# Two-block transformer kernel: order of loads, place of selection rounds and form of the reciprocals in the layer attention

## The reference

```python
h = rms_norm(x); proj = h @ w_in                       # 1024 x 3528
mixed = concat(retention(ret_cols),                    # 4 heads, chunkwise, with a norm and a gate
               dsa(dsa_cols),                          # 4 heads
               dilated(dil_cols))                      # 8 heads
x = x + mixed @ w_out
x = x + square(relu(rms_norm(x) @ w_up)) @ w_down

# dsa: every query attends to the 128 keys with the best index score
logits = einsum('bqhd,bsd->bqhs', q_idx, k_idx)        # 8 index heads
score  = einsum('bqhs,bqh->bqs', relu(logits), w_idx)  # causal mask after it
_, idx = top_k(score, 128)
p = softmax(q @ k[idx] * 64 ** -0.5); o = p @ v[idx]
```

## Time and profile before

| what | us |
|---|---|
| median of three runs | 3216.89 |
| profiled execution | 3215.07 |
| its span | 3213.0 |
| TensorE matmul busy | 2753.3 (86%) |
| VectorE busy | 1742.8 (54%) |
| ScalarE busy | 1271.9 (40%) |
| first layer of the second block: index sums to end of projections | about 1700 to 1857 |
| its layer attention, first scores | 1873.7 |

### The profile page before, as it was taken

How to read it: one execution, slowest core, us unless ns; L and a number is a source line. 1 busy time by engine, 2 the same in 40 slices (tenths; PEclk the granted TensorE clock), 3 DMA queues, 4 the chain that set the end, 5 groups by cost and what they waited for, 6 DMA issues and landing times. The chain is left out here.

```text
span 3213.0 us, 34356 instructions
## 1 busy us (share of the span) xinstructions
PE 2753.3 (86%) x11967; PEld 2064.3 (64%) x11967; DVE 1742.8 (54%) x2583; ACT 1271.9 (40%) x1739; POOL 114.6 (4%) x172
## 2 busy tenths in 40 slices
PE   3879989978798399999489969899999996989998
PEld 0167566556577277777376746688877573668886
DVE  1045146667575588888635755444443665544444
ACT  1033246656522177777433245222233314532222
POOL 2011000000000100000000100000000100000000
PEclk9989999989999699999779979899997997989999
DMA  8655343245253299999622442122222234222221
GB/s 316 217 159 151 114 109 91 81 103 129 90 180 118 111 354 371 386 371 366 232 61 82 118 109 85 62 95 91 91 87 63 92 99 129 65 66 92 95 100 72
DMA packets 241592, 466.35 MB, mean 145 GB/s; under 512 B 67864, under 2 KB 90640, under 8 KB 241455
## 3 DMA queue, kind: packets, MB, share of 16 engines
q1 hardware_dynamic: 226383, 413.73, 39.2%
q0 software_dynamic: 15072, 50.87, 4.7%
HBM read 399.83 MB, written 64.72 MB: 145 GB/s over the span
## 5 line engine op out<-in xcount | busy, mean ns | idle before, releaser
L1803 DVE TENSOR_TENSOR WL<-W,WH 128x2048 fp32r<-128x2048 f32 x131 | 300.2, 2292 | 502.2 <-ACT WH L1275 497.0
L1275 ACT ACTIVATE WH<-W 128x2048 fp32r<-128x2048 f32 x131 | 250.4, 1912 | 649.8 <-PE BKP L736 590.1
L736 PE MATMUL BKP<-hH,WH 128*128 128x512 f32 x896 | 357.4, 399 | 15.8 <-DVE hL L2201 13.2
L736 PE MATMUL BKP<-hL,WH 128*128 128x512 f32 x896 | 352.7, 394 | 0.0
L736 PE MATMUL BKP<-hH,WL 128*128 128x512 f32 x896 | 352.7, 394 | 0.0
L736 PE MATMUL BKP<-WH,aH 128*128 128x512 f32 (+1 forms) x544 | 215.3, 396 | 22.5 <-DVE aL L2396 10.4
L736 PE MATMUL BKP<-WL,aH 128*128 128x512 f32 (+1 forms) x544 | 211.4, 389 | 0.0
L736 PE MATMUL BKP<-WH,aL 128*128 128x512 f32 (+1 forms) x544 | 211.3, 388 | 0.0
L736 PEld LDWEIGHTS BKP<-hH,WH 128*128 128x128 f32 x896 | 171.4, 191 | 57.1 <-issue 20.3
L736 PE MATMUL BKP<-WH,hH 128*128 128x512 f32 (+3 forms) x512 | 201.2, 393 | 7.2 <-ACT Z L1326 3.1
L736 PE MATMUL BKP<-WH,hL 128*128 128x512 f32 (+3 forms) x512 | 194.2, 379 | 0.0
(11 more groups left out here) (443 smaller groups left out, 5581.1 us busy)
## 6 DMA issues: line engine op xcount, KB each, us to landing
W<-in_w_expert_gu_dram SPq DMA_DIRECT2D x46, 1024.0 KB, 8.7
G<-in_w_expert_gu_dram SPq DMA_DIRECT2D x46, 1024.0 KB, 8.9
W<-in_w_in_dram SPq DMA_DIRECT2D x42, 1024.0 KB, 5.4
W<-in_w_up_dram SPq DMA_DIRECT2D x32, 1024.0 KB, 5.4
W<-in_w_down_dram SPq DMA_DIRECT2D x32, 1024.0 KB, 5.0
W<-in_w_expert_down_dram SPq DMA_DIRECT2D x24, 1024.0 KB, 8.0
G<-in_w_expert_down_dram SPq DMA_DIRECT2D x22, 1024.0 KB, 8.0
X<-in_w_in_dram SPq DMA_DIRECT2D x16, 1024.0 KB, 8.2
```

The costliest lines, as they stand in the source:

```text
L736: mm = pe.matmul(BK[j][:, 0:cols], lt, rh, start=start and a == 0, stop=stop and a == len(q) - 1, skip_group_check=True)
L1275: act.activation(WH[s][:], W[s][:], ACT.Copy).then_inc(sems["w_hi"], 1)
L1803: v.tensor_tensor(WL[s][:], W[s][:], WH[s][:].bitcast(F32), ALU.subtract).then_inc(sems["w_lo"], 1)
```

## The change

Four edits, all in the second block's layers:

1. SyncE's wait for the stores moves from the front of `mixed_heads` to behind the loads of the first two heads, in front of the two w_out loads. What the first heads load was stored long before, and retention's own loads have waited for it.
2. ScalarE rounds the first head (`mixed_rounded(0)`) during the evacuation of the last projection unit, in front of the copy of part 2. A tiny exponential in front of it brings the table of the exponential in at that place. VectorE makes that head's remainders (`mixed_remainders(0)`) in front of `selected(3)`. `sel_done` goes: TensorE's first scores don't need the selection, and VectorE, which adds the mask, has made it itself.
3. Eight rounds of tile 2 move behind the index sums 16 to 23. In the loop of 24 steps there remain eight rounds of tile 2 (steps 0 to 7) and 16 of tile 3 (steps 8 to 23), one a step.
4. VectorE writes a head's reciprocals out as 64 equal columns (two copies), for both heads side by side. TensorE spreads them once for a pair, after the second head's product, with 128 weight columns.

```diff
-TOP_2 = [2, 2, 1, 2, 1, 2, 2, 1, 2, 1]
-TOP_3 = [1] * 12 + [2] * 2
+TOP_2 = [1] * 8
+TOP_3 = [1] * 16
...
+        TINY = F[:, 1, 16:17]
+        RDW = [AT[:, c:c + 256].rearrange("p (t s c) -> p t s c", t=2, s=2) for c in (512, 1280)]
...
             def after_retention(s):
-                if s == 0:
-                    for b in range(3):
-                        sp.wait_ge(sems[f"st_written{b}"], T.next(f"st_written{b}", stored(STORES_2, b)))
-                        sp.sem_inc(sems["paused"], 1)
                 sp.wait_ge(sems["ret_oe"], T.next("ret_oe", NT))
...
                 for s in range(2):
                     values(4 + s, s)
+                for b in range(3):
+                    sp.wait_ge(sems[f"st_written{b}"], T.next(f"st_written{b}", stored(STORES_2, b)))
+                    sp.sem_inc(sems["paused"], 1)
                 for u in range(2):
                     load(WOR[u], out_unit(wo, 0, u), ...)
...
-                    pe.wait_ge(sems["head_rd"], T.next("head_rd"))
-                    for tt in range(NT):
-                        mm = pe.matmul(RD2[rows, tt * P:(tt + 1) * P], RDS[:, s, tt:tt + 1].to_broadcast([P, HD]), IDN[:], ...)
+                    if s == 1:
+                        pe.wait_ge(sems["head_rd"], T.next("head_rd", 2))
+                        for tt in range(NT):
+                            mm = pe.matmul(RD2[:, tt * P:(tt + 1) * P], RDW[tt // 2][:, tt % 2, :, :]..., IDN[:], ...)
...
-                pe.wait_ge(sems["sel_done"], T.next("sel_done"))
                 mixed_attention()
...
-                gemm(copies(lambda j: ST[1][:, j, :], UN, 4, "st_filled1"), None, False)
-                act.wait_ge(sems["sel_done"], T.next("sel_done"))
+                def first_head(j):
+                    if j == 2:
+                        act.activation(TINY, IDN[:, 0:1], ACT.Exp)
+                        mixed_rounded(0)
+                gemm(copies(lambda j: ST[1][:, j, :], UN, 4, "st_filled1", first_head), None, False)
...
-                    v.reciprocal(RDS[:, s, :], DENS[:, s, :]).then_inc(sems["head_rd"], 1)
+                    link(v.reciprocal(RDS[:, s, :], DENS[:, s, :]))
+                    for half in range(2):
+                        ins = v.tensor_copy(RDW[half][:, :, s, :],
+                                            RDS[:, s, 2 * half:2 * half + 2].unsqueeze(2).to_broadcast([P, 2, HD]))
+                    ins.then_inc(sems["head_rd"], 1)
...
                         if n >= 8:
                             top_rounds(1, 1)
+                        if n >= 16:
+                            top_rounds(2, 1)
...
-                        top_rounds(2, TOP_2[q]) if q < 10 else top_rounds(3, TOP_3[q - 10])
-                        if q == 9:
+                        top_rounds(2, TOP_2[q]) if q < 8 else top_rounds(3, TOP_3[q - 8])
+                        if q == 7:
                             selected(2)
...
+                mixed_remainders(0)
                 selected(3)
-                v.sem_inc(sems["sel_done"], 1)
```

More of the change, by code:

```diff
@@ L958, in values @@
                     for kt in range(NT):
-                        pe.matmul(OT2[rows, kt * P:S], VS[s][:, kt, :], PT2[s][:, kt, kt * P:S], start=kt == 0,
+                        mm = pe.matmul(OT2[rows, kt * P:S], VS[s][:, kt, :], PT2[s][:, kt, kt * P:S], start=kt == 0,
                                   stop=kt == NT - 1, skip_group_check=True)
-                    pe.wait_ge(sems["head_rd"], T.next("head_rd"))
-                    for tt in range(NT):
-                        mm = pe.matmul(RD2[rows, tt * P:(tt + 1) * P], RDS[:, s, tt:tt + 1].to_broadcast([P, HD]), IDN[:], start=True, stop=True,
-                                       skip_group_check=True)
+                    if s == 1:
+                        pe.wait_ge(sems["head_rd"], T.next("head_rd", 2))
+                        for tt in range(NT):
+                            mm = pe.matmul(RD2[:, tt * P:(tt + 1) * P], RDW[tt // 2][:, tt % 2, :, :].rearrange("p s c -> p (s c)"), IDN[:],
+                                           start=True, stop=True, skip_group_check=True)
                     mm.then_inc(sems["head_o"], 1)
@@ L1479, in attend, with mixed_rounded @@
                 T.skip("head_o:free", 2)
+            def mixed_rounded(s):
+                act.wait_ge(sems[f"qk_landed{s}"], T.next(f"qk_landed{s}", 64))
+                act.activation(QX[s], QS[s][:], ACT.Copy)
+                act.activation(KX[s][:, 0:S], KS[s][:, 0:S], ACT.Copy).then_inc(sems["head_hi"], 1)
             def mixed_attention():
[L1483 to L1486, removed]
                 def exponential(n):
@@ L1521, in body @@
                         if tt == 0 and not (last and s == 1):
-                            rounded(1 - s)
+                            mixed_rounded(1 - s)
                         if tt == 0:
@@ L1533, in mixed_attention @@
                 act.sem_inc(sems["head_ptc"], 2)
-                rounded(0)
                 exponential(0)
@@ L2076, in _, with mixed_remainders @@
             attend(8, lambda tt: KEYS, None, to_stage(1), 0, beside=conv_taps(0))
-            def mixed_attention(chosen, dilated, beside):
[L2080 to L2084, removed]
+            def mixed_remainders(s):
+                v.wait_ge(sems["head_hi"], T.next("head_hi"))
+                v.tensor_tensor(QX[s][HD:P, :], QS[s][HD:P, :], QX[s][HD:P, :].bitcast(F32), ALU.subtract)
+                v.tensor_tensor(KL[s][:, 0:S], KS[s][:, 0:S], KX[s][:, 0:S].bitcast(F32),
+                                ALU.subtract).then_inc(sems["head_lo"], 1)
+            def mixed_attention(chosen, dilated, beside):
                 def top(n, bias):
@@ L2146, in body @@
                         if tt == 1 and not (last and s == 1):
-                            remainders(1 - s)
+                            mixed_remainders(1 - s)
                         if n == 1 and not first:
@@ L2155, in mixed_attention @@
                 T.skip("head_o", 2)
-                remainders(0)
                 top(0, chosen)
```

## The result

The changed kernel took 3222.56 us (median of 20 runs) against 3215.68 for the kernel before on the same chip (20 runs). The ratio is 1.0021, 95% interval 1.0013 to 1.0028: 6.8 us slower. I had forecast 3211.2 us, that is faster by 5.7, with a range up to 3222.

What follows compares the result with a forecast made beforehand. TensorE was taken to bound the kernel. Rounds +10.2, seam net -9.7 and reciprocals -3.4 gave -2.9 us per layer, -5.7 for both; 3215.07 became 3209.4, plus 1.8 for the median: 3211.2 us, range 3199 to 3222.

Steps and rivals of the forecast that it cites:

- The rounds: Index sums to retention: moved rounds make TensorE wait 7.4 us more before transposes, 2.8 before retention scores; +10.2 per layer.
- the upper end of a range: Cost of the moved rounds per layer, 9.5 to 12 us; the upper end is for more time at the lower clock.
- The load's place in the queue: Before the retention scores: head loads, queued behind the delayed next weights, land at 1794.5; TensorE waits another 2.8 us.
- the signs that I had named as right: TensorE waits 11.5 us before transposes, 2 to 4 before retention scores, 3 to 4 before layer attention; ScalarE 4 to 6.
- The seam: Between projections and layer attention: first scores at 1860.95 instead of 1873.69; gain 12.7 us per layer, net -9.7.
- The third head: Layer attention: its loads stand behind the store wait and w_out, so 3.0 us per layer come back (2 to 5).
- rival 2: SyncE's queue takes gain back: late retention loads, stores stretched 3 us, late heads; +4.1 per layer, 3225 us; chance 0.14.
- The 2 us more: Stores and new head loads take turns on the DMA engines before layer attention, making it some 2 us worse per layer.
- The table load: ScalarE's last projection evacuations: 1.28 us, costed at nothing; at 2.66 us the sum would be some 2.6 us worse.
- The reciprocals: Layer attention: one spreading group fewer per pair of heads, 12 of 24 go; -3.4 us per layer (-5.8 to -2).
- The sum: Whole kernel: +10.2 - 9.7 - 3.4 = -2.9 us per layer, -5.7 for both layers.

Runs made afterwards that it cites:

- the better version: Changed kernel without rounds on the index sums, two tile-2 rounds in each of the first eight steps, w_out loaded behind third and fourth heads' loads: 3191.06 us.

## Why the prediction was wrong

**The rounds: the term that failed.** I had +10.2 per layer; it is +14.1 (28.2 us over both by the medians; 14.1 and 13.9 in the profiles, up to the end of the projections). The mechanism was right, and the sizes were off at its end. The chain shifts the transposes by 1778.71 - 1766.05 - 5.30 = 7.36 us (figured 7.4). The next weights go out at 1790.27, which is 1785.0 on the clock of the kernel before (figured 1784.9), and the last retention load at 1790.2 (figured 1789.9). It takes 5.4 us to land, not the 4.6 of before, so the retention scores start at 1795.6 on that clock where I had 1794.5: 1.1 us of the miss. (TensorE comes there 0.8 us later than by the chain alone, through the lower clock in the unit ahead, so its wait is 3.2; without that it would be 4.0 for the 2.8 that I had.) The larger part is what I left to the upper end of a range, "for more time at the lower clock", and so put at nothing in the sum: 2.8 us from the retention scores to the end of the projections (76.0 us for 73.2), which is where the slow unit lies. 10.2 + 1.1 + 2.8 = 14.1. I had one such stretch in my own rows, half clock behind the 16 us wait, and the transposes at 1.97 us behind the 4.09 us wait; the new wait should have had one too, priced by the passes behind it. The load's place in the queue, which I had figured as 2.8, is worth 6.1 when it is taken away.

Nearly all the signs that I had named as right came: waits before the transposes (9.4 us, not 11.5, as the product and the transposes between them take 1.8 us longer at the lower clock), 3.2 before the retention scores, 3.42 before the first scores, 4.14 on ScalarE at the third head. They show the mechanism and not the sum.

**The seam: right in what it gains.** Gain 12.75 (16.17 to 3.42 between the end of projections and the first scores), figured 12.7. The third head gives back 2.4 at its scores, figured 3.0, and more behind them, as the run with w_out later shows. w_out was issued at 1886.16, which is 1866.7 on the clock of the kernel before (the ends of the projections lie 19.42 apart), figured 1866.8. Before, the wait for the stores was over by 1865.8, so the stores beside the new loads took some 0.9 us longer, for the 1 that I had taken and the 3 of rival 2. The 2 us more that I had worked out from the Trainium skill's rule of turns between rings (DMA: Bandwidth & Descriptors, Queues, rings and completion order) didn't come. The table load cost nothing: it ended 1.54 us before ScalarE's bank was there. So this place can't tell 1.28 us from the 2.66 of the Trainium skill (ScalarE: Activation LUTs, What ACT_TABLE_LOAD costs). The seam alone measured -8.7 per layer for my -9.7; two rounds still stand behind the last copy there, so 1.7 us of the figured gain are not in it. In the +14.1 of the rounds, which comes from the medians, this gain is counted, and against it the third head, whose scores come 19.1 us behind the first scores in the changed kernel and 17.2 in the run without the rounds.

**The reciprocals: over-rated.** I had -3.4 per layer; alone they measured -0.8 (the interval allows -1.9). The passes go as figured, but the group that stays lasts 1.16 us instead of 1.04, so a pair saves 0.88 us and not 1.0, and in the profile this is seen at the last three pairs only. Two things give it back. VectorE's two copies stand on the chain of the first pairs, +0.4 at each of two. And in the first layer the stretches at the lower clock are longer at one place and new at another. The new one lies behind the last head, where TensorE waits 1.91 us for VectorE's remainder instead of 1.72:

```profile
1997.05 0.49 PE L982 MATMUL BKP<-aH,hH 128*128 128x512 f32 x1 [1.91 <-DVE hL L2112]
1997.38 0.40 PE L983 MATMUL BKP<-WL,hH 128*128 128x512 f32 x1
...
1998.51 0.63 PE L984 MATMUL SCP<-WH,hL 128*128 128x512 f32 x1
```

```profile
1990.00:2010.00 20.00, 18.09 (x75) 13.85 (x74) 7.66 (x12) 3.01 (x6) 0.00 (x0) 0.91 0.31 105
1905.00:1930.00 25.00, 20.31 (x72) 12.27 (x71) 12.43 (x35) 13.08 (x35) 0.00 (x0) 0.71 0.34 94
```

0.91 over 20 us where the same stretch before has 1.00, and 0.71 around the third pair where it was 0.89. Eight passes at 0.63 cost 8 x 0.2 = 1.6 us, nearly twice what a saved group is worth. The stretch at the end comes with the spread reciprocals, and this the profiles of all runs show. In the nine kernels that have them, the 20 us from 122 us behind the first scores have a granted clock of 0.91 in 15 of 18 layers, and from the last values product to the transposes it takes 40.9 us there and 39.3 in the other three layers, of which the second layer of this kernel is one. In the four kernels without them all eight layers have 1.00 and 39.05 us. Why three layers escape it no run shows. For the third pair it isn't shown: from the second pair's last values product to the third's it takes 22.6 and 21.6 us with the reciprocals alone and 20.6 and 21.4 before, but 19.5 and 20.8 with them in the better version and 20.3 and 20.6 without.

**The sum.** +14.1 - 8.7 - 0.8 is +4.6 per layer, +9.2 for both; measured +6.8. My -5.7 differs by +7.8 for the rounds, +2.0 for the seam and +5.2 for the reciprocals. By the stages of the profile two sums failed, each by 3 to 4 us per layer: up to the end of the projections it is +14 for my +10.2, and in layer attention +3.3 and +2.8 for my -0.4. Rival 2 had nearly the right time, 3225, by luck: the retention loads went out 0.3 us later than figured and landed 1.1 later, not 2, the stores weren't stretched by 3 us, and the loss behind the retention loads is for the greater part the clock's.

## What to carry to other kernels

Price a new wait of the bounding engine with the passes behind it: here a 3.2 us wait came with 2.8 us of slower passes behind it. Before work is moved onto a chain that ends in a buffer's release, look at what stands behind that release on the load queue, and put small loads that are needed soon ahead of a large one. And where a load sets the time, a faster engine ahead of it only waits longer: try the two cures together, not one after the other. Passes that only keep the engine busy must stand where it really waits: in the better version 18 of them stood where it waited 0.30 us, and delayed the chain by 4.0.

## What was not expected of the hardware

The granted clock stayed at 1.2 GHz for 17 us in and behind two waits of 4.2 and 5.2 us that stood 4 us apart, counted from the end of the first, and 6.9 us behind one of 3.2. Behind the same single wait of 4.09 us, with the same passes, it was 6.6 us in the first layer and 10.2 in the second of the kernel before, so such a stretch has no one price. Forty passes whose results nobody reads brought the first of these from a mean of 0.72 to 0.94 or 0.99; the time was 6 us less in one kernel, at the edge of what can be told, the same in another, and no less in the better version, though its mean clock there was 1.00. And saving one group of eight passes in a pair brought a stretch of 1.2 GHz at another place, worth 1.8 us, in 15 of 18 layers.
